# Projecting v inside the recurrence, a head pair at a time, with native fp32 products

## The reference, cut to what matters

```python
dx = h_prev - h
r, k, v = einsum('sbtc,scd->sbtd', h[None] + dx[None] * mu[:3, None, None, :], w_rkv)
...
y = wkv7_scan(heads(r), heads(decay), heads(k), heads(v), -kk, kk * a_h)
...
bonus = sum(heads(r) * heads(k) * r_k, axis=-1, keepdims=True)
y = y + (bonus * heads(v)).reshape(B, T, C)
return (y * g) @ w_o
```

## Time and profile before

| what | value |
|---|---|
| median of 3 runs | 3390.49 us (3390.43 to 3415.55) |
| the profiled execution: its own time | 3388.53 us |
| its span in the trace | 3386.7 us |
| mean granted TensorE clock in it | 0.949 of full |
| PE busy | 3149.7 us, 93% of the span |
| DVE, ACT, POOL busy | 1666.8, 1149.6, 142.1 us |

### The profile page before, as it was taken

The page is one execution under the profiler, slowest core; times in us unless marked ns, Lnnn a source line. Parts: engine busy times, 40 slices in busy tenths (PEclk is TensorE's granted clock), DMA queues, the critical chain, the costliest instruction groups (busy, mean ns, idle before and its releaser), DMA issues.

```text
span 3386.7 us, 39065 instructions
## 1 busy us (share of the span) xinstructions
PE 3149.7 (93%) x15716; PEld 2508.4 (74%) x15716; DVE 1666.8 (49%) x2751; ACT 1149.6 (34%) x1853; POOL 142.1 (4%) x145
## 2 busy tenths in 40 slices
PE   7999889899998889999999999769999989988998
PEld 6888567666667768888788888548888767877886
DVE  5434543456655654344754345775535435245235
ACT  4222133344444333223332224453323333233332
POOL 0000000211211100000000000000000000000000
PEclk9999999799999999999999999779999989987999
DMA  4333232000000033333233332003333110201231
GB/s 127 97 96 94 63 111 75 27 28 28 28 28 15 1 118 100 99 94 100 75 100 94 99 97 88 1 22 101 96 94 95 61 38 1 85 13 47 85 96 56
DMA packets 173896, 234.77 MB, mean 69 GB/s; under 512 B 14201, under 2 KB 111062, under 8 KB 173462
## 3 DMA queue, kind: packets, MB, share of 16 engines
q1 hardware_dynamic: 173718, 232.29, 22.1%
HBM read 228.05 MB, written 4.19 MB: 69 GB/s over the span
## 4 chain that ended last, share of the span: by engine, by line
PE 84%; DVE 9%; ACT 4%; issue 2%; POOL 1%; DMA 0%; SPq 0%; DVEq 0%; ACTq 0%
PE banks L830 63%; PE banks L1317 3%; PE banks L972 2%; PE banks L1311 1%; PE banks L963 1%; PE banks L1305 1%; PE banks L1007 1%; PE banks L1034 1%; PE banks L940 1%; PE banks L1030 1%; PE banks L981 1%; DVE diff_scores L2316 1%; DVE diff_small L2322 1%; PE banks L918 1%; ACT L1556 1%
## 5 line engine op out<-in xcount | busy, mean ns | idle before, releaser
L1865 DVE TENSOR_TENSOR weights_lo<-weights_raw,weights_hi 128x1024 fp32r<-128x1024 f32 (+2 forms) x393 | 472.8, 1206 | 1038.2 <-ACT weights_hi L1388 1036.9
L830 PE MATMUL banks<-operand_hi,weights_hi 128*128 128x512 f32 x2208 | 873.0, 395 | 28.3 <-DVE weights_lo L1865 14.5
L830 PE MATMUL banks<-operand_lo,weights_hi 128*128 128x512 f32 x2208 | 865.9, 392 | 0.0
L830 PE MATMUL banks<-operand_hi,weights_lo 128*128 128x512 f32 x2208 | 865.6, 392 | 0.0
L1388 ACT ACTIVATE weights_hi<-weights_raw 128x1024 fp32r<-128x1024 f32 (+2 forms) x393 | 407.9, 1041 | 1090.9 <-PE banks L830 1049.5
L830 PEld LDWEIGHTS banks<-operand_hi,weights_hi 128*128 128x128 f32 x2208 | 418.4, 189 | 123.2 <-issue 25.8
L830 PEld LDWEIGHTS banks<-operand_lo,weights_hi 128*128 128x128 f32 x2208 | 418.9, 190 | 88.6 <-issue 2.2
L830 PEld LDWEIGHTS banks<-operand_hi,weights_lo 128*128 128x128 f32 x2208 | 418.3, 189 | 88.3
L972 PE MATMUL banks<-operand_lo 128*128 128x512 f32 x370 | 173.2, 492 | 1.3 <-ACT v L1508 1.3
L830 PE MATMUL banks<-hidden_ffn_hi,weights_hi 128*128 128x512 f32 x352 | 137.1, 390 | 0.0
L830 PE MATMUL banks<-hidden_ffn_hi,weights_lo 128*128 128x512 f32 x352 | 136.9, 389 | 0.0
(11 more groups left out here) (509 smaller groups left out, 4424.7 us busy)
## 6 DMA issues: line engine op xcount, KB each, us to landing
weights_raw<-in_ffn_w_in_dram SPq DMA_DIRECT2D x352, 256.0 KB, 3.0
weights_raw<-in_ffn_w_out_dram SPq DMA_DIRECT2D x88, 512.0 KB, 3.7
weights_raw<-in_w_in_dram SPq DMA_DIRECT2D x36, 512.0 KB, 3.6
weights_raw<-in_rwkv_w_rkv_dram SPq DMA_DIRECT2D x24, 512.0 KB, 3.8
weights_raw<-in_w_mod_dram SPq DMA_DIRECT2D x24, 512.0 KB, 4.9
weights_raw<-in_w_kv_dram SPq DMA_DIRECT2D x16, 512.0 KB, 3.6
weights_raw<-in_rwkv_w_o_dram SPq DMA_DIRECT2D x8, 512.0 KB, 5.3
weights_raw<-in_diff_w_q_dram SPq DMA_DIRECT2D x8, 512.0 KB, 4.3
```

The costliest lines, as they stand in the source:

```text
L830: mm = nc.tensor.matmul(o, l, r, start=first and t == 0 and job["opens"], stop=last and t == 2, **skip)
L1865: nc.vector.tensor_tensor(ring_lo[0:p, u["slot"], 0:n, 0:w], ring_raw[0:p, u["ring"], 0:n, 0:w], f32(ring_hi[0:p, u["slot"], 0:n, 0:w]), A ...
```

## The change

The dense pass of v is gone. DVE makes the mixed operand of v as plain fp32 while k's first block runs and keeps it where v was (`mixed_v`). Each pair m gets one direct unit of weights, all 1024 rows of its 128 columns (512 KB in pieces of 512 B). PE makes eight native fp32 products (128 x 128 weights, 512 tokens) into bank 7, in the filling slot of eight places, in place of idle products. ACT copies the result to `v_of_pair`, a buffer for two pairs. The modulation products of a pair follow in the places after that copy. The readers of v (the transposes of `x` at level 4, and the bonus in `gh`) wait for the copy. `w`, a buffer of the recurrence, moves into the room of `operand_hi` to make space. The products of v stand at the pair's places +3, +6, ... +24 (`decay` to `x` at level 1 of half 0; for pair 0, whose lane is alone there, at 3, 4, ... 10), the copy at +25 (11), and the modulation products at +26, +29, ... +47 (12 to 24).

```diff
-        for s in range(3):
+        for s in range(2):
             layer["rkv", s] = dense(I["rwkv_w_rkv"][0, s])
...
+            layer["v", m] = plan(C, [([columns(I["rwkv_w_rkv"][0, 2], m * P, m * P + P)], P)], direct=True, nk=KC)
...
-        for m in range(MOD_BLOCKS):
-            room = starts[m + 1] - starts[m] - 8
+        for m in range(KC):
+            first, v_used = starts[m] + 3, WKV_ORDER.index((lane_of[m, 0], m, 0, ("x", 4)))
+            apart = min(3, (v_used - 3 - first) // (KC - 1))
             for k in range(KC):
-                FILL[starts[m] + 3 + k * room // KC] = ("mod", m, k)
...
+                FILL.setdefault(first + k * apart, []).append(("v", m, k))
+            kept = first + (KC - 1) * apart + 1
+            FILL_ACT.setdefault(kept, []).append(("v", m))
+            if m < MOD_BLOCKS:
+                room = starts[m + 1] - 4 - kept
+                for k in range(KC):
+                    FILL.setdefault(kept + 1 + k * room // KC, []).append(("mod", m, k))
...
+                else:
+                    uid = layer["v", n][0][0]
+                    if k == 0:
+                        pe.wait_ge(*arrived[units[uid]["ring"]].at(uid))
+                        if n == 0:
+                            pe.wait_ge(*mixed_made.at(("v", KC - 1)))
+                        else:
+                            pe.wait_ge(*(fill_dve.at(("mod", n - 1)) if n <= MOD_BLOCKS else fill_act.at(("v", n - 1))))
+                    mm = nc.tensor.matmul(ps[:, MISC_BANK], joined(ring_raw[:, units[uid]["ring"]])[:, k * P:(k + 1) * P],
+                                          rkv[2][:, k], start=k == 0, stop=k == KC - 1)
+                    if k == KC - 1:
+                        mm.then_inc(*fill_pe.by(("v", n, k)))
...
+                        if lv == 4:
+                            pe.wait_ge(*fill_act.at(("v", m)))
...
+                    if kind == "v":
+                        nc.scalar.activation(v_[:, n % 2], ps[:, MISC_BANK], ACT.Copy).then_inc(*fill_act.by(("v", n)))
...
+                                nc.vector.scalar_tensor_tensor(out=rkv[2][:, k], in0=dx[:, k],
+                                                               scalar=vec("rwkv_mu", 2 * KC + k), in1=h[:, k, 1:T + 1],
+                                                               op0=ALU.mult, op1=ALU.add).then_inc(*mixed_made.by(("v", k)))
```

More of the change, by code:

```diff
@@ L966, in pairs @@
                         mm.then_inc(*by_pe.by(at(f"{use}{e}")))
-                if place in FILL:
-                    modulation_rows(*FILL[place])
-                else:
+                for job in FILL.get(place, ()):
+                    between(*job)
+                if place not in FILL:
                     nc.tensor.matmul(ps[:, IDLE_BANK], two_ident, two_ident.unsqueeze(1).broadcast_to([P, 4, P]),
@@ L1518, in act_program @@
             for place, (lane, m, half, step) in enumerate(WKV_ORDER):
-                if place in FILL and FILL[place][0] == "mod" and FILL[place][2] == KC - 1:
-                    n = FILL[place][1]
-                    act.wait_ge(*fill_pe.at(("mod", n, KC - 1)))
-                    nc.scalar.activation(row[:, :], ps[0:2, MISC_BANK], ACT.Copy).then_inc(*fill_act.by(("row", n)))
+                for kind, n in FILL_ACT.get(place, ()):
+                    act.wait_ge(*fill_pe.at(("v" if kind == "v" else "mod", n, KC - 1)))
+                    if kind == "v":
+                        nc.scalar.activation(v_[:, n % 2], ps[:, MISC_BANK], ACT.Copy).then_inc(*fill_act.by(("v", n)))
+                    else:
+                        nc.scalar.activation(row[:, :], ps[0:2, MISC_BANK], ACT.Copy).then_inc(*fill_act.by(("row", n)))
                 L = Lane(lane, m, half)
@@ L2033, in dve_program @@
             for place, (lane, m, half, step) in enumerate(WKV_ORDER):
-                if place in FILL and FILL[place][0] == "turn":
-                    n = 4 * FILL[place][1]
-                    dve.wait_ge(*fill_pe.at(("turn", n // 4)))
+                for kind, i in FILL_DVE.get(place, ()):
+                    n = 4 * i
+                    dve.wait_ge(*fill_pe.at(("turn", i, 0)))
                     nc.vector.tensor_tensor(mod[:, n:n + 4, :], ps[:, MISC_BANK, 0:8].rearrange("p (i j) -> p i j", j=2),
                                             vecs[:, nb + n:nb + n + 4].unsqueeze(2).broadcast_to([P, 4, 2]),
-                                            ALU.add).then_inc(*fill_dve.by(("mod", n // 4)))
+                                            ALU.add).then_inc(*fill_dve.by(("mod", i)))
                 L = Lane(lane, m, half)
@@ L2639, in sp_program @@
                         direct_done[uid] = done_in(lane_pe, m, 0, use)
+            for m in range(KC):
+                direct_done[layer["v", m][0][0]] = fill_pe.at(("v", m, KC - 1))
             for n in range(MOD_BLOCKS):
@@ L2671, in sp_program @@
             nc.sync.dma_start(x_kept, x[:, :, :]).then_inc(*x_spilled.by(0))
-            weights(through(("g2", KC - 1)) + AHEAD)
+            weights(through(("v", KC - 1)) + AHEAD)
             for sem, value in ends["wkv"]:
```

79 lines of the change are left out of this document (47 added, 32 removed).

## The result

The changed kernel takes **3352.56 us** (median of 4 runs, 3348.68 to 3357.76) against 3396.03 us for the kernel before on the same chip (4 runs, 3390.43 to 3415.55). The ratio is 0.9863, with a 95% interval of 0.9818 to 0.9908. The forecast was 3360.5 us, with a range of 3338 to 3386. The profiled execution took 3348.68 us, the fastest of the four, and its span is 3346.8 us at a mean granted clock of 0.957. Of the 35 runs of the kernel before on record, 14 took 3412 us or more and the other 21 took 3402 or less, so its median hangs on their mix, while none of the ten runs of the changed kernel is above 3358.39 us.

What follows compares the result with a forecast made beforehand. PE was taken as the bound, with 84% of the chain that ended last. Terms -42.9 + 20.6 + 5.5 + 5 - 18 = -29.8 us took 3388.5 to 3358.7, 3360.5 at the median; range 3338 to 3386.

Steps and rivals of the forecast that it cites:

- The pass of v: Dense pass of v: its 192 products go and the mixing on DVE stays covered, -42.9 us.
- The price of a product: Recurrence: each of v's 64 native products adds 0.84 us to PE's queue over an idle one, 53.8 us in all.
- The hidden share: Recurrence: five of a pair's eight v products lie under waits, three do not; with pair 0, +20.6 us.
- the sixth product: v's product at `x` level 0 of a pair, hidden in front of the 1.74 us wait for POOL.
- the fifth and the seventh: v's products at `pairs` and `d` level 0 of a pair: no cover, 0.84 us each.
- The modulation products: Pairs 0 to 5: pressed into the second part, 1.5 more uncovered products a pair, +5.5 us.
- Copy and load: Recurrence: ACT's copy of v, 0.4 us for each of 8, and waits for v's weights in pairs 2 and 5, +5 us.
- the third rival: v's weights late at each `decay`, 22 us in all, time near 3380; chance 0.13, shared with a clock not recovering.
- The clock: Recurrence: v's products fill waits, so most low-clock falls in first parts of pairs go, -18 us (0 to -35).
- The sum: Whole kernel: all terms together -29.8 us, 3360.5 us at the median; recurrence from 609 to about 622 us.
- a sign of being wrong: Recurrence does not grow: uncovered products or clock misjudged; growth over 30 us would mean the waits moved along.
- The first rival: Recurrence swallows all of v's products and stays at 609 us; gain 42.9 to some 50, time 3340 to 3347; chance 0.24.

Runs made afterwards that it cites:

- the native products beside the pass: Kernel before with v's pass kept, modulation products moved and 64 native products added whose result nobody reads; 3387.73 us against 3395.76, ratio 0.9952.
- the second profile: Profiled execution, slowest of six, of the unchanged changed kernel measured again; 3347.49 us against 3394.36 for the kernel before, ratio 0.9857.

## Why the prediction was right, point by point

**The pass of v.** Forecast -42.9 us, measured -42.4 and -39.4 (the starts of the recurrence, 539.0 and 542.0 against 581.4). The mixing on DVE cost PE nothing.

**The price of a product.** Forecast 0.84 us over an idle product, measured 0.62. This is the term that was mis-sized: 1.06 us was read from products behind which the shape of the weights changes. The total is 40 us and not 53.8. The 0.09 us that a modulation product's 2 columns add can be had back by making it wide.

**The hidden share.** Forecast five of eight hidden and 20.6 us on the path. Measured at equal clock: 14 us for 56 products and 16 for 64, in two comparisons. So about 60% was hidden, as forecast, and the term comes out smaller for the price of a product above all. The share is right in part by luck, since the map of the places was read from pair 6 and taken for seven pairs. In pair 6 it holds. The three waits of the earlier trace rows, 1.37, 1.63 and 1.74 us, are in the changed kernel

```profile
977.21 0.67 PE L1016 MATMUL banks<-x_turned,headsum 128*128 128x256 f32 x2 [0.70 <-ACT x_turned L1580]
...
985.66 0.46 PE L1137 MATMUL banks<-a_nv,n_q 128*128 128x128 f32 x2 [0.49 <-DVE a_nv L2188]
...
995.40 0.63 PE L1036 MATMUL banks<-operand_hi 128*128 128x128 f32 x4 [1.11 <-POOL operand_hi L2617]
```

They gave up 0.67, 1.14 and 0.63 us, the price of four products. In pairs 1 and 4 the kernel before has no wait for POOL in the first half, and in pairs 2 and 5 none for ACT at `decay`. So in pair 1 the sixth product, forecast as hidden, was on the path in full, and the fifth and the seventh, forecast as uncovered, cost little or nothing; its seven products cost 0.8 us in all. The evidence for the products in DVE's stretch had a flaw too: pair 7's 13.60 us, against pair 4's 12.40, stood at a clock of 0.87, 3.5 us of low clock, and these are about the whole difference. It still shows no cost of the three.

**The modulation products.** Forecast +5.5 us, measured some 2 at equal clock over the whole recurrence, and 0.8 in pair 3. (The forecast took 1.1 us five times, though pairs 0 to 5 are six.)

**Copy and load.** Forecast +5 us. The matmuls waited for v's weights twice, 0.5 us in all: 0.28 us in pair 2 and 0.19 in pair 5, the two pairs that the forecast named. With their weight loads, which wait beside them, the view of the line has 1.8:

```profile
  DMA weights_raw<-in_rwkv_w_rkv_dram: 1.8, 5
```

In pair 2, where `decay` follows close on `lora`, the unit was issued and used as follows (SP's queue and PE):

```profile
669.78 0.37 SPq L2673 DMA_DIRECT2D weights_raw<-in_rwkv_w_rkv_dram  x1
...
673.89 0.70 PE L969 MATMUL banks<-mixed_v,weights_raw 128*128 128x512 f32 x1 [0.28 <-DMA weights_raw<-in_rwkv_w_rkv_dram]
```

PE could use the 512 KB in pieces of 512 B 4.1 us after their issue, as fast as the modulation unit's 4.0, and not at the window bias's 6.8. That refutes the third rival. The copy does stand in front of the square, as the order said:

```profile
632.62 0.60 ACT L1553 ACTIVATE v_of_pair<-banks 128x512 f32<-128x512 f32 x1
633.10 0.52 ACT L1580 ACTIVATE x_turned<-k,vectors 128x256 f32<-128x256 f32 x1
```

It delays the square by 0.48 us; pair 1 took 70.7 us without copy and load (the native products beside the pass) and 71.2 with them. And the first modulation product of pair 2 stood 0.83 us (the row at 706.97 above), until the copy was over, which ran from 706.27 to 706.87. As an estimate from these two figures, that is 4 to 6 us in eight pairs.

**The clock.** Forecast -18 us, with pairs 1 to 5 free of low clock and under 20 us of it in pair 0. Measured 30 and 47 us of it in place of 91: 3 and 17 us in pairs 1 to 5 (25 before), so the second profile is not free of it there, 7 and 14 us in pair 0, and 16 and 13 in pair 7, where it was expected to stay. At 0.36 to 0.45 us each that is 16 to 28 us.

**The sum.** Forecast +13 us for the recurrence, measured -1.1 and +5.1. Pair 3 took 78.9 us for a forecast of 79, pair 6 75.3 for 77. The terms as measured add to 15 + 2 + 5 less 16 to 28, which is +6 to -6. The prediction named a sign of being wrong, a recurrence that does not grow, and in the first profile it did not, in the second it grew by 5.1 us. What it said of such a case is what the runs show: the uncovered products were misjudged, at 20.6 us for some 15, and the modulation products with them, at 5.5 for 2, and the clock gave back about as much as forecast, or more. (Its last addition is off by a little as well: 3358.7 + 2.0 is 3360.7, not 3360.5.)

**The first rival.** It had the recurrence cost nothing net, a gain of 42.9 us to some 50 and 3340 to 3347 us. The gains of 43.5 and 46.9 us lie in its span and 14 to 17 us above the forecast's 29.8, and beside the pass the native products cost 0.6 us net. So for the size of the gain this rival was nearer than the forecast. As to how, the runs side with the forecast: nothing net is the sum of some 15 us on the path and as much back from the clock, and where the clock gave little back, the cost shows. Neither 8 more products in the second half of each of pairs 6 and 7 nor a second one behind each of v's was swallowed.

What is open: why the granted clock falls in one execution of a kernel and not in the next. 132 and 78 us of low clock came from the same instructions. The runs show only that fuller waits go with less of it: 78 to 132 us in the five profiles without products of v or others in their place, 28 to 47 in the nine with them.

## What to carry to other kernels

Read the price of an instruction that is to be moved from a row in which its neighbours are alike, above all in the shape of their weights; the same product read between other shapes was a quarter dearer. A map of waits holds for the pairs in which the lanes stand to each other in the same way: read it for each kind of pair, and look further than the next wait, as a later one can pay too. And before a stage's time is compared, its granted clock is: at equal instructions the recurrence moved by 24.5 us with it here, more than the change's whole effect on that stage.

## What the chip showed beyond that

A native fp32 product with 512 moving columns took 0.86 us from start to start with 128 by 128 weights among neighbours of the same shape, 0.95 with 2 columns of weights, and 1.06 between weights of 64, 128 and 32 rows. Filling waits can cost less than nothing: with 56 products less the kernel was 11 us slower, and its recurrence had 98 us of low clock in place of 30 to 47.
